# Prediction and experiments: cached latent pages turned by transfers and VectorE instead of TensorE

## The reference, cut to what matters

```python
def step(carry, phys):                       # one page of each sequence
    c_blk = cache_ckv[layer, phys]           # 128 positions x 256 latent numbers
    kp_blk = cache_kpe[layer, phys]          # 128 positions x 32 rotary numbers
    kn_blk, v_blk = _decompress(c_blk, w_ukv, g_kn)   # kn = rmsnorm over 64 numbers of each of 8 heads
    return _merge(carry, _attn_partial(qn, qp, kn_blk, kp_blk, v_blk, None)), None
```

## Time and profile before

| quantity | value |
|---|---|
| median of the timed runs | 1332.03 us (1331.44 to 1332.09) |
| the profiled execution | 1327.66 us |
| its span from first to last instruction | 1325.6 us |
| mean granted TensorE clock | 0.981 of full |
| PE busy | 1271.7 us, 96% |
| DVE, ACT, POOL busy | 716.2, 455.3, 152.7 us |
| transfers | 82995 packets, 81.48 MB |

### The profile page before, as it was taken

The page is one execution under the profiler, slowest core; times in us unless marked ns, Lnnn a source line. Parts: engine busy times, 40 slices in busy tenths (PEclk is TensorE's granted clock), DMA queues, the critical chain, the costliest instruction groups (busy, mean ns, idle before and its releaser), DMA issues. The chain is left out here.

```text
span 1325.6 us, 25998 instructions
## 1 busy us (share of the span) xinstructions
PE 1271.7 (96%) x9479; PEld 740.7 (56%) x9479; DVE 716.2 (54%) x1781; ACT 455.3 (34%) x1108; POOL 152.7 (12%) x182
## 2 busy tenths in 40 slices
PE   6999999889999999999999989999999999989898
PEld 4545677656666666655545545665545455454343
DVE  4001448654566656565767776777666666530331
ACT  3001354233343434342445433343444444310320
POOL 0000326400010202024302320000000000000000
PEclk9999999899999999998999998999999999999899
DMA  6422121111111111310331114311333212001000
GB/s 213 161 79 54 34 64 33 52 38 33 30 36 44 39 32 39 74 50 20 93 101 46 41 37 133 131 38 37 103 119 111 79 55 71 34 0 36 16 16 36
DMA packets 82995, 81.48 MB, mean 61 GB/s; under 512 B 18947, under 2 KB 76612, under 8 KB 82869
## 3 DMA queue, kind: packets, MB, share of 16 engines
q1 hardware_dynamic: 80452, 73.87, 18.5%
q10 hardware_dynamic: 2416, 5.96, 1.3%
HBM read 75.72 MB, written 4.07 MB: 60 GB/s over the span
## 5 line engine op out<-in xcount | busy, mean ns | idle before, releaser
L499 PE MATMUL PS<-wk,c_T 128*128 128x512 f32 x1024 | 494.5, 606 | 0.0
L624 DVE TENSOR_REDUCE ssq<-sq__69 128x8 f32<-128x512 f32 x256 | 175.2, 684 | 183.1 <-ACT sq__69 L553 181.9
L499 PEld LDWEIGHTS PS<-wk,c_T 128*128 128x128 f32 x1024 | 176.6, 192 | 152.0 <-issue 139.6
L553 ACT ACTIVATE sq__69<-PS 128x512 f32<-128x512 f32 x256 | 152.6, 596 | 315.8 <-PE PS L499 315.3
L1482 PE MATMUL PS<-xnT,w_ring 128*128 128x276 f32 x416 | 102.6, 404 | 0.0
L1320 PE MATMUL PS<-w_ring,xnT 128*128 128x424 f32 x256 | 95.7, 531 | 0.9 <-DVE xnT L976 0.9
L1482 PEld LDWEIGHTS PS<-xnT,w_ring 128*128 128x128 f32 x416 | 78.9, 193 | 21.2 <-issue 4.1
L455 PE MATMUL PS<-cst,c_ring 128*128 128x128 f32 x512 | 79.6, 278 | 6.1 <-DVE dots_s L619 4.7
L455 PEld LDWEIGHTS PS<-cst,c_ring 128*128 128x128 f32 x512 | 60.3, 143 | 44.7 <-issue 40.2
L1320 PEld LDWEIGHTS PS<-w_ring,xnT 128*128 128x128 f32 x256 | 48.7, 194 | 45.3 <-issue 45.2
L2690 PE MATMUL PS<-w_g,nT 128*128 128x512 f32 x128 | 56.0, 594 | 0.0
(11 more groups left out here) (533 smaller groups left out, 1872.1 us busy)
## 6 DMA issues: line engine op xcount, KB each, us to landing
c_ring<-in_cache_ckv SPq DMA_DIRECT2D x256, 128.0 KB, 2.8
w_ring<-in_w_in SPq DMA_DIRECT2D x4, 1696.0 KB, 12.5
w_ring<-in_w_in SPq DMA_DIRECT2D x9, 512.0 KB, 5.1
r_ring<-in_cache_kpe SPq DMA_DIRECT2D x256, 16.0 KB, 1.8
w_o<-in_w_out SPq DMA_DIRECT2D x8, 512.0 KB, 4.2
w_g<-in_w_ple_gate SPq DMA_DIRECT2D x8, 512.0 KB, 3.6
xn<-in_x_prompt SPq DMA_DIRECT2D x4, 512.0 KB, 11.0
w_ring<-in_w_in SPq DMA_DIRECT2D x2, 1024.0 KB, 6.0
```

Source lines behind the costliest of these rows:

```text
L499: mm = pe.matmul(PS[:, NORM[v % 2], :], c_T[:, u % 2, k, t * P:(t + 1) * P], wk[:, k], start=(k == 0), stop=(k == 1))
L553: nc.scalar.activation(sq_[:, v % 2, :], PS[:, NORM[v % 2], :], ACT.Square).then_inc(no_sb, 1)
L624: dve.tensor_reduce(ssq[:, u % 2, t * H:(t + 1) * H], sq_[:, v % 2, :].rearrange("p (h c) -> p h c", h=H), AX.X, ALU.add).then_inc(red_sb, 1)
```

## The change

- A page's turn no longer runs on PE. Once the pages of a step are in `c_ring`, four transfers within SBUF (`latent_blocks`) gather, for each quarter g of the 256 latents, that quarter of all 512 positions onto 32 partitions of a new tile `c_blocks`. Each moves 128 KB, in pieces of 64 numbers (256 bytes). SP issues quarters 0 and 1, ACT quarters 2 and 3, for the step after next of what ACT computes; there is one `c_blocks`, freed by `ct_sb`.
- DVE turns `c_blocks` in blocks of 32 x 32 with two transposes of 128 x 512 into one of two `c_T` buffers. The latents stand in another order on the partitions, so `wk` is loaded in the same order by eight transfers instead of being cut out of `wukv` by ACT.
- ACT squares in place, in PSUM, and DVE sums from there. norms(v) now waits for the reduce of v - 2.
- The copy of the scores (`dotted`) moves from DVE in slot 1 to ACT in slot 3, with one buffer instead of two.
- `RING` is 5, `ahead_pages` 2, `PREP_SLOTS` 2: three slots move from the preparation into the tail stretch.
- In the last stage the samples' turn stands ahead of the gate product of tile 0, and `mixed(3)` ahead of `normed(1)`, `given(0)` and `added(2)`.

```diff
@@ -129,7 +129,7 @@
-RING = 4
+RING = 5
@@ -137,7 +137,7 @@
-PREP_SLOTS = 5
+PREP_SLOTS = 2
...
+        def latent_blocks(eng, u, groups_c):
+            eng.wait_ge(c_in[u % RING], 16 * GT * (u // RING + 1))
+            if u >= 1:
+                eng.wait_ge(ct_sb, u)
+            for g in groups_c:
+                eng.dma_start(c_blocks[32 * g:32 * g + 32].rearrange("p x t c -> p (x t c)"),
+                              c_ring[:, slot_of[u], :, g * (KVL // 4):(g + 1) * (KVL // 4)]).then_inc(b_in, 16)
+
         def pages_sp():
             sp = nc.sync
...
+            for u in range(NSTEP + 1):
+                if u < NSTEP:
+                    page = page_numbers(u)
+                    if u >= RING:
+                        sp.wait_ge(vv_ps, u - RING + 1)
+                        sp.sem_inc(slot_taken, 1)
+                    if u >= ahead_pages:
+                        latent_pages(u, page)
+                if u >= 3:
+                    latent_blocks(sp, u - 1, (0, 1))
...
-            def turn_c(u, k):
-                if k == 0:
-                    pe.wait_ge(c_in[u % RING], 16 * GT * (u // RING + 1))
-                    if u >= 1:
-                        pe.wait_ge(rp_sb, u)
-                else:
-                    pe.wait_ge(k0_sb, u + 1)
-                for t in range(GT):
-                    mm = pe.transpose(PS[:, TURN, t * P:(t + 1) * P], c_ring[:, u % RING, t, k * P:(k + 1) * P], ident)
-                mm.then_inc((k0_ps, k1_ps)[k], 1)
-
             def turn_r(u):
                 pe.wait_ge(r_in[u % R_RING], 16 * GT * (u // R_RING + 1))
-                pe.wait_ge(k1_sb, u + 1)
+                if u >= 1:
+                    pe.wait_ge(rp_sb, u)
                 pe.transpose(PS[:, TURN, 0:P], r_ring[:, u % R_RING, :], ident).then_inc(tn_ps, 1)
...
                 if t == 0:
-                    pe.wait_ge(k1_sb, u + 1)
+                    pe.wait_ge(ct_sb, u + 1)
                 if v >= 2:
-                    pe.wait_ge(no_sb, v - 1)
+                    pe.wait_ge(red_sb, v - 1)
...
+            def dotted(u):
+                if u >= 1:
+                    act.wait_ge(eq_sb, u)
+                act.wait_ge(rp_ps, u + 1)
+                nc.scalar.copy(dots_s[:].rearrange("p x c -> p (x c)"), PS[:, TURN, P:3 * P]).then_inc(rp_sb, 1)
+
             def square(u, t):
                 v = u * GT + t
-                if v >= 2:
-                    act.wait_ge(red_sb, v - 1)
                 act.wait_ge(no_ps, v + 1)
-                nc.scalar.activation(sq_[:, v % 2, :], PS[:, NORM[v % 2], :], ACT.Square).then_inc(no_sb, 1)
+                nc.scalar.activation(PS[:, NORM[v % 2], :], PS[:, NORM[v % 2], :], ACT.Square).then_inc(no_sb, 1)
...
-            turned_c(0)
+            latent_blocks(act, 0, range(4))
             yield
+            latent_blocks(act, 1, range(4))
             yield
...
-                if t == 2 and ahead:
-                    turned_c(u + 1)
-                if t == 3 and u >= 1:
-                    weights(u - 1)
+                if t == 3:
+                    if u >= 1:
+                        weights(u - 1)
+                    dotted(u)
+                if t == 2 and u + 2 < NSTEP:
+                    latent_blocks(act, u + 2, (2, 3))
                 square(u, t)
...
             def turned_c(u):
-                dve.wait_ge(k1_ps, u + 1)
-                dve.tensor_copy(c_T[:, u % 2, 1, :], PS[:, TURN, :]).then_inc(k1_sb, 1)
...
+                dve.wait_ge(b_in, 16 * 4 * (u + 1))
                 if u >= 2:
-                    dve.wait_ge(eq_sb, u - 1)
...
+                    dve.wait_ge(rp_ps, u - 1)
+                    dve.wait_ge(no_ps, (u - 1) * GT)
+                for k in range(2):
+                    ins = dve.transpose(c_T[u % 2][:, k].rearrange("p (t a x) -> p t x a", t=GT, x=GT),
+                                        c_blocks[:].rearrange("p x t (k c) -> p k t x c", k=2)[:, k])
+                ins.then_inc(ct_sb, 1)
...
+                    if n == 2:
+                        sp.wait_ge(xT_ps, NT + 1)
+                        for g in range(4):
+                            for k in range(2):
+                                c0 = g * (KVL // 4) + 32 * k
+                                nope = io["w_ukv"][c0:c0 + 32, :].rearrange("i (h c) -> i h c", h=H)[:, :, 0:NOPE]
+                                sp.dma_start(wk[32 * g:32 * g + 32, k].rearrange("p (h c) -> p h c", h=H), nope
+                                             ).then_inc(wk_in, 16)
```

More of the change, by code:

```diff
@@ L251, in build @@
         ms = place("ms", [P, 4])
+        turned_at = place.at
+        c_T0 = place("c_T0", [P, 2, GT * P])
         ring_at = place.at
-        c_T = place("c_T", [P, 2, 2, GT * P])
+        c_ring = place("c_ring", [P, RING, GT, KVL + 1])
+        blocks_at = place.at
+        c_blocks = place("c_blocks", [P, GT, GT, KVL // 4])
+        c_T = c_T0, place("c_T1", [P, 2, GT * P])
+        rope_at = place.at
         r_T = place("r_T", [P, P])
@@ L415, in page_numbers @@
             b, j = divmod(u, STEPS)
-            return [nc.sync.value_load(pages[0:1, (j * BS + b) * GT + x:(j * BS + b) * GT + x + 1], min_val=0,
-                                       max_val=io["cache_ckv"].shape[0] - 1) for x in range(GT)]
+            return [nc.sync.value_load(pages[0:1, (j * BS + b) * GT + x:(j * BS + b) * GT + x + 1]) for x in range(GT)]
         def latent_pages(u, page):
@@ L516, in pages_pe @@
                         values(u - 2)
-                if t == 2:
-                    if ahead:
-                        turn_c(u + 1, 0)
-                    if u >= 1:
-                        turn_scale(u - 1)
-                if t == 3 and ahead:
-                    turn_c(u + 1, 1)
+                if t == 2 and u >= 1:
+                    turn_scale(u - 1)
                 norms(u, t)
@@ L665, in pages_dve @@
                 ahead = u + 1 < NSTEP
-                if t == 0 and u >= 1:
-                    scales(u - 1)
+                if t == 0:
+                    if u >= 1:
+                        scales(u - 1)
                 if t == 1:
-                    dotted(u)
+                    if ahead:
+                        turned_c(u + 1)
                     if u >= 2:
@@ L2764, in _ @@
                 projected(2, 1)
+                pe.wait_ge(mt_act, 3)
+                pe.wait_ge(mt_dve, 3)
+                pe.wait_ge(own_sb, 1)
+                s_turn(s_rows[:, C_GA:NAT], OUT_M, ms_ps)
                 gated(0, 0)
                 gated(0, 1)
[L2767 to L2769 removed]
+                mixed(3)
                 normed(1)
[L2771 removed]
                 pe.wait_ge(x1_sb, 3)
@@ L2917, in _ @@
                 dve.tensor_tensor(gate, PS[0:NS, MISC, :], gate, ALU.mult).then_inc(own_sb, 1)
-                given(0)
-                added(2)
                 dve.wait_ge(ms_ps, 1)
                 dve.tensor_copy(msT[:, 4:8, :], turned_of(OUT_M + 1, NS)).then_inc(ms_dve, 1)
+                given(0)
+                mixed(3)
+                added(2)
                 turned_n(1)
-                mixed(3)
                 dve.wait_ge(os_ps, 1)
@@ L3018, in _ @@
                 ins.then_inc(at_sb, 1)
+                act.wait_ge(ms_ps, 1)
+                nc.scalar.copy(msT[:, 0:4, :], turned_of(OUT_M, NS)).then_inc(ms_act, 1)
                 gated(0)
+                mixed(3)
                 act.preload_act_table_set(LN_EXP)
                 added(2)
-                act.wait_ge(ms_ps, 1)
-                nc.scalar.copy(msT[:, 0:4, :], turned_of(OUT_M, NS)).then_inc(ms_act, 1)
                 turned_n(1)
-                mixed(3)
                 act.wait_ge(os_ps, 1)
```

93 lines of the change are left out of this document (35 added, 58 removed).

## The result

The changed kernel took 1345.38 us (median of 4 runs, 1343.5 to 1350.11) against 1332.06 for the kernel before beside it: a ratio of 1.0111, 95% interval 1.0089 to 1.0133. It is 1.1% slower; 1286 was forecast, with a range up to 1312. The profiled execution took 1346.85 us with a span of 1345.0 (before 1325.6).

The account below looks back on a forecast made before the run. PE, busy 96% of the span, was taken to bound the kernel. Against the profiled 1327.66 us, -37.7 + 2 - 12.6 + 6 - 3 = -45.3 gave 1282, plus 4.4 for the timed median 1286; range 1262 to 1312.

Parts of the forecast that it names:

- DVE ... In time: Tail step, DVE's queue: merge ends at 5.2 us, the reduce of slot 1 at 6.36, judged in time for slot 3's norms.
- n2: Tail step: start of the norms of slot 2 on PE, put at 4.97 us after the start of slot 0's norms.
- this chain: Tail step: the waits that set its length; transposes of 0.68 us assumed off it, coming onto it at 0.9.
- the forecast's 9.19: Tail stretch: a step falls from 9.76 to 9.19 us, which over 22 steps gives 12.6 us.
- The wait for the score copy: Tail step: turn_r waits for ACT's score copy, starting at about 8.95 us instead of 8.41.
- C: Rival, slow transposes: at 1.25 us each a tail step is 9.85 and the total 1303; chance 0.12.
- The attention, +2 forecast: Prompt attention: transposes put some 0.9 us more into one DVE slot; 0.25 us given back in 8 steps, 2 us.
- 3 for the start: Start of the stage after preparation: ACT, held by page numbers and four loads, delays PE for some 3 us.
- Forecast +2.9 in preparation and moved slots together: Preparation: next stage starts 4 us earlier; three slots moved to the tail stretch cost 6.9 there, together +2.9.
- The end: Last stage: with the new order s_groups starts near 1234.7 instead of 1237.84, gain 3 us, between 0 and 6.
- PE busy about 60 us less: Whole kernel: a sign named in advance that the forecast holds, PE's busy time down by about 60 us.
- rival D: Transfers within SBUF land late: beyond 6 us each us lengthens a tail step by one; 1375 at 10 us; chance 0.09.

Follow-up runs that it names:

- a1: The changed kernel with VectorE's merge put ahead of the two transposes in slot 1: 1320.38 us, ratio 0.9921.
- a2: The changed kernel without VectorE's transposes from the third step on, only their signal given: 1312.6 us, one execution.
- a4: The changed kernel with transposes writing side by side, rotary keys and weights permuted to match: 1337.03 us, ratio 1.0059.
- e1: The changed kernel with the merge ahead of the transposes and, in the prompt attention alone, ScalarE's square ahead of issues and score copy: 1313.92 us, ratio 0.9871.
- d1: The changed kernel with the merge ahead of the transposes and, in all stages, ScalarE's square ahead of issues and score copy: 1336.66 us, ratio 1.0056.
- e2: The changed kernel with the merge ahead of the transposes and, in all stages, only ScalarE's two issues put behind the square: 1320.8 us, ratio 0.9926.
- b1: The kernel before with only the squares left in PSUM, squared in place and summed from there: 1325.71 us, ratio 0.9963.
- b3: The kernel before with only the new order of the last stage: 1328.37 us, ratio 0.9975.
- b2: The kernel before with only PREP_SLOTS 2 instead of 5, moving three slots into the tail stretch: 1332.32 us, ratio 1.0026.
- a3: The changed kernel without the block transfers from the third step on, transposes kept: 1322.3 us, one execution.

## Why the prediction was wrong

**The step that failed is "DVE ... In time".** In the tail step I let the merge end at 5.2 us and compared it only with the sum of slot 1, and put n2 at 4.97. But n2 has `turn_scale` ahead of it, and that waits for the merge. By my own numbers it was already 0.5 late; with the pair of transposes at 2.01 us and the merge at 0.42, as the trace has them, the merge ends at 5.74 (3.31 + 2.01 + 0.42), and L487, due at 4.7, is 1.04 late: the trace shows 0.85 and 1.09. The claim that transposes come onto this chain only at 0.9 us was false: by the same numbers they are on it from 0.46 ((4.7 - 3.31 - 0.475) / 2). a1 shows that the wait is real, and that with it gone the tail stretch is 223.2 us against the 220.9 forecast.

**That its step of 9.2 us is the forecast's 9.19 is luck in part.** In the shortest steps of a1 and a2 PE waits for nothing that the trace shows, and they take 8.92, that is 9.76 less 0.84. I had 8.65, since I took the 0.23 us before turn_r for a wait; it is there in steps without one too (the trace of before has 0.07 us idle there). The wait for the score copy was forecast as 0.54 in each step and is 0.46 in about every second one. The two errors offset each other.

**Transposes.** 1085 ns, inside my bounds (0.4 to 1.25) and nearer to C, whose reason, a stride of 4 elements, a4 confirms. C's price of 1303 missed the same wait, so even the right duration would have left me 40 us short.

**The attention, +2 forecast beside -7.8, +15.9 measured,** is the largest mis-sized term: 21.7 us. I charged the transposes 0.25 us a step, and nothing for the issues or the copy, without a reason. ScalarE is busy 50.91 of 131 us there, but its idle time said nothing: it sits in a closed loop. The four parts read from the intervals, transposes 0.96, issues 0.53, copy 0.41 and pairing 0.24, come to 2.1 a step, of which 0.2 overlap: 15.5 us in 8 steps. That e1 returns the middle two is shown (intervals of 3.71 and 3.81; 135.9 us for 144.7); the copy's share is shown by d1 against e2 (3.80 against 4.21).

**Stages ahead of it.** The recurrence came out as forecast, by luck: -12.6 was 15.6 of slots less 3 for the start, and that 3 never showed (270.6 us in a1 and 270.1 in a2, that is -15.8 and -16.2). In its place L487 waited 3.8 us for the merge. The samples' recurrence (+8.4 for -5.5) has PE idle 6.2 us more and a granted clock of 0.88 for 0.95; without transfers it takes 105.9 at 0.94, with dense transposes and the merge first 107.5 at 0.95. But b1 and b3, with none of these, take 110.1 at 0.92, and b3 has the code of before in this stage, so some 3 us of it come and go between executions with the clock. Of the latents' 11.4 us, 6.1 go with the merge; the rest has no experiment of its own.

**Start and end.** Forecast +2.9 in preparation and moved slots together, measured -2.7 and +6.6 (b2): +3.9. The end gave 1.5 of 3. Of the signs, "PE busy about 60 us less" failed as well: it is 35.5.

**Right:** the landing of the transfers (3.9 to 4.5 us for a load of such pieces, 4.3 and 4.9 here), so that rival D did not happen. Yet by a3's one execution the transfers cost 23 us: 9.4 in the samples' recurrence, 5.6 in the tail stretch, 5.4 in the attention, 3.0 in the latents. Only the attention's part is traced, to ScalarE's issues. Squares in PSUM cost nothing (b1), and the Trainium skill's larger fixed cost of a PSUM read (VectorE: DVE Perf Modes, the section on the TRN2 errata) again does not show: the sum from PSUM takes 687 ns, and from SBUF it took 0.68 us.

## What to carry over

When work is put into an engine's queue, list everything that stands behind it in that slot and, for each, who waits for it, through shared PSUM banks too; comparing the queue with its next known deadline is not enough. Put what releases another engine ahead of long work that has slack, and decide it for each stage: the order that gave 7 us back in the attention cost 18.6 in the tail. An idle share tells nothing about an engine inside a closed loop; the interval between two starts of the same instruction does. And when a layout is changed to speed up one engine, price the reads and writes of all the others that share it.

## What the runs showed of the hardware

- A VectorE transpose of 128 x 512 float32 in 32 x 32 blocks: 1085 ns with an output stride of 4 elements, 686 ns with blocks side by side, the same as a sum over as many elements (687).
- A float32 matmul of 128 x 128 on TensorE: 296 ns a record with its moving operand side by side, 411 with a stride of 4 elements (after, a4). An exponential of 128 x 128 on ScalarE: 389 ns, and 511 when it writes with a stride of 4.
- 512 KB moved within SBUF as four transfers, each from 128 partitions onto 32 in pieces of 256 bytes: each lands 4.3 (issued by ScalarE) or 4.9 us (SyncE) after its issue, in the median. The rotary keys, loaded in the same kernel, need 3.8 us instead of 1.8; without these transfers 1.7.
- ScalarE squares a bank in place in 583 ns. An issue of such a transfer holds its queue for 0.66 us in the median (0.63 and 0.66 in the rows above).
